# A mixer turn's three weight splits change place, and one na-gate piece on TensorE moves from attention tile 1 to tile 0

## What is computed

```
xr, kx, vx, gx, qx, mrx, mnx = split(modulate(x) @ w_in)
cr, kc, vc                   = split(modulate(ctx) @ w_in[:, :3072])
h        = rglru_bidirectional(conv4(xr), conv4(cr))        # gated recurrence, both directions
y_rnn    = h * gelu(gx)
y_na     = neighborhood_attention(rope(rms(qx)), rms(qx), rope(rms(kx)), vx, rms(kc), vc, rpb)
x        = x + m2 * ((sigmoid(mrx) * (y_rnn @ w_rnn_out) + sigmoid(mnx) * (y_na @ w_na_out)) @ w_out)
x        = x + m5 * conv_ffn(modulate(x))
```

## Time and profile before

| | |
|---|---|
| median of 3 runs | 2131.47 us (2130.02 to 2133.41) |
| the profiled execution | 2128.76 us, of which the span from first to last instruction is 2126.9 us |
| granted TensorE clock | 0.997 of full speed |
| TensorE busy | 2051.1 us (96% of the span) |
| DVE, ACT, GpSimd busy | 1628.0 (77%), 1072.5 (50%), 492.8 us (23%) |
| a stretch of 141 us over one middle turn (501 to 642 us) | TensorE 138.59 us busy, DVE 107.06, ACT 91.47, GpSimd 30.87 |

### The profile page before, as it was taken

How to read it: one execution, slowest core, us unless ns; L and a number is a source line. 1 busy time by engine, 2 the same in 40 slices (tenths; PEclk the granted TensorE clock), 3 DMA queues, 4 the chain that set the end, 5 groups by cost and what they waited for, 6 DMA issues and landing times.

```text
span 2126.9 us, 28320 instructions
## 1 busy us (share of the span) xinstructions
PE 2051.1 (96%) x10618; PEld 1739.8 (82%) x10618; DVE 1628.0 (77%) x2809; ACT 1072.5 (50%) x1631; POOL 492.8 (23%) x377
## 2 busy tenths in 40 slices
PE   5999999999999999999998899999999999999999
PEld 1878888988988889888887788887788888887887
DVE  6688598596885985859859866767998888877766
ACT  3466666665676657656666621002444334434332
POOL 0031130222212212212123010000124442115550
PEclk9999999999999999999999999999999999999999
DMA  8421211112012120120111385453347764239663
GB/s 328 112 64 41 62 51 47 47 53 70 30 41 72 40 73 20 53 70 30 43 50 69 106 310 193 144 188 131 89 134 197 183 176 118 94 122 335 226 205 126
DMA packets 105576, 241.65 MB, mean 114 GB/s; under 512 B 27264, under 2 KB 32768, under 8 KB 104960
## 3 DMA queue, kind: packets, MB, share of 16 engines
q1 hardware_dynamic: 74304, 191.08, 26.4%
q0 software_dynamic: 14592, 44.05, 8.0%
q10 hardware_dynamic: 16544, 4.72, 1.0%
HBM read 203.11 MB, written 63.96 MB: 126 GB/s over the span
## 4 chain that ended last, share of the span: by engine, by line
PE 77%; DVE 13%; ACT 4%; issue 2%; ACTq 0%; DVEq 0%
PE banks L47 14%; PE banks L49 14%; PE banks L48 14%; PE banks L991 4%; PE banks L862 4%; PE banks L864 4%; PE banks L863 4%; PE banks L895 3%; PE banks L2269 3%; PE banks L2270 3%; PE banks L2271 3%; DVE probT_low L1494 2%; PE banks L953 2%; DVE prob L1486 2%; PE banks L935 1%
## 5 line engine op out<-in xcount | busy, mean ns | idle before, releaser
L47 PE MATMUL banks<-qh,xnh 128*128 128x384 f32 (+1 forms) x640 | 223.3, 349 | 0.3 <-PEq L216 0.3
L862 PE MATMUL banks<-xnh,wh 128*128 128x512 f32 (+1 forms) x536 | 211.3, 394 | 3.2 <-ACT stage L1097 2.9
L49 PE MATMUL banks<-qh,xnl 128*128 128x384 f32 (+1 forms) x640 | 207.7, 325 | 0.0
L48 PE MATMUL banks<-ql,xnh 128*128 128x384 f32 (+1 forms) x640 | 207.6, 324 | 0.0
L864 PE MATMUL banks<-xnh,wl 128*128 128x512 f32 (+1 forms) x536 | 204.5, 381 | 0.0
L863 PE MATMUL banks<-xnl,wh 128*128 128x512 f32 (+1 forms) x536 | 204.1, 381 | 0.0
L1494 DVE TENSOR_TENSOR probT_low<-banks,probT_high 128x512 fp32r<-128x512 f32 (+2 forms) x256 | 138.9, 583 | 56.2 <-ACT probT_high L1165 55.2
L1165 ACT CAST probT_high<-banks 128x512 fp32r<-128x512 f32 (+2 forms) x256 | 117.0, 510 | 60.3 <-PE banks L953 51.4
L47 PE MATMUL banks<-yh,wh 128*128 128x512 f32 x372 | 145.0, 390 | 0.9 <-DVE wl L2471 0.9
L48 PE MATMUL banks<-yl,wh 128*128 128x512 f32 x372 | 145.0, 390 | 0.0
L49 PE MATMUL banks<-yh,wl 128*128 128x512 f32 x372 | 144.9, 390 | 0.0
(11 more groups left out here) (396 smaller groups left out, 6015.9 us busy)
## 6 DMA issues: line engine op xcount, KB each, us to landing
raw<-w_ff SPq DMA_DIRECT2D x33, 512.0 KB, 5.7
down_d<-w_down POOLq DMA_DIRECT2D x66, 256.0 KB, 6.9
raw<-w_fm SPq DMA_DIRECT2D x32, 512.0 KB, 6.7
extras<-h_d SPq DMA_DIRECT2D x55, 256.0 KB, 3.9
raw<-w_qkv SPq DMA_DIRECT2D x24, 512.0 KB, 3.9
raw<-w_mix SPq DMA_DIRECT2D x24, 512.0 KB, 4.8
h_d<-conv_d SPq DMA_DIRECT2D x21, 512.0 KB, 3.2
raw<-w_modT SPq DMA_DIRECT2D x16, 512.0 KB, 4.6
```

Of the source, the lines that this page charges most:

```text
L47: pe.matmul(out, w_hi(k), x_hi(k), start=(k == 0), stop=False)
L48: pe.matmul(out, w_hi(k), x_lo(k), start=False, stop=False)
L49: last = pe.matmul(out, w_lo(k), x_hi(k), start=False, stop=(k == chunks - 1))
L862: pe.matmul(out, fh[:, s, k, :], xnh[:, k, c0:c1], start=(k == 0), stop=False)
```

## The change

In `turn` of the five programs:

- In turns 1 to 6 the splits of XR and MR stand earlier: on ACT after the evacuation and gates of q tile 1, on DVE after `head_squares` of q tile 1.
- In turns 0 to 6 the MN split stands earlier: on ACT in front of the evacuation of MR's first half, on DVE between the normalisation of the last queries and `maxima` of tile 0. Before it stood behind the high parts of `JOBS_B` on ACT and behind their low parts on DVE.
- In turn 7 the MN split goes to q tile 1 on both engines, and `LAST_ORDER` puts MN in front of MR, with SP's wait changed to MR.
- On TensorE the piece after the scores at u = 1 is gone, and one after the scores at u = 0 is new (turns 0 to 6).

```diff
@@ -587,7 +587,7 @@
         SLOT = {XR: 0, G: 1, MR: 1, MN: 0}
         RAW = {Q0: 0, Q1: 1, Q2: 2, XR: 0, MR: 1, MN: 2, G: 0}
         ORDER = {Q0: 0, Q1: 1, Q2: 2, XR: 3, MR: 4, MN: 5, G: 6}
-        LAST_ORDER = {Q0: 0, Q1: 1, Q2: 2, MR: 3, MN: 4}
+        LAST_ORDER = {Q0: 0, Q1: 1, Q2: 2, MN: 3, MR: 4}
 
         def split_count(u, i, last=False):
             return i * UNITS + 2 + (LAST_ORDER if last else ORDER)[u] + 1
@@ -747,7 +747,7 @@
                     store_stage(smr_d, i, 1, 1)
                     store_stage(smn_d, i, 0, 2)
                     sp.wait_ge(yr_out, PAIRS * 16)
-                    sp.wait_ge(w_lo, split_count(MN, i, True))
+                    sp.wait_ge(w_lo, split_count(MR, i, True))
                     for k in range(2):
                         load_y(k)
                     sp.dma_start(raw[:, 2, :], w_mix[0]).then_inc(mix_in, 16)
@@ -1072,7 +1072,7 @@
                         mix_piece((u - 5) // 2)
                     if u + 2 < ATT:
                         scores(i, u + 2)
-                    if not last and u % 2 == 1 and u < ATT - 1:
+                    if not last and (u == 0 or u % 2 == 1 and 1 < u < ATT - 1):
                         piece()
                     if u % 2 == 0 and u >= 2:
                         weighted_values(i, u // 2 - 1)
@@ -1222,6 +1222,8 @@
                     for s in range(1, 4):
                         q_evac(i, s)
                         gate_pieces(i, *GATES_LAST[s])
+                        if s == 1:
+                            split_hi(MN, raw_count(MN, i))
                     decays(i, 0)
                     q_evac(i, 4)
                     root(i, 0)
@@ -1233,6 +1235,9 @@
                     for s in range(3):
                         q_evac(i, s, first)
                         gate_pieces(i, *GATES_AFTER[s])
+                        if s == 1:
+                            split_hi(XR, raw_count(XR, i))
+                            split_hi(MR, raw_count(MR, i))
                     decays(i, 0)
                     q_evac(i, 3)
                     q_evac(i, 4)
@@ -1240,11 +1245,10 @@
                     gate_pieces(i, *GATES_AFTER[4])
                     q_evac(i, 5)
                     gate_pieces(i, *GATES_AFTER[5])
-                if not last:
+                if first:
                     split_hi(XR, raw_count(XR, i))
-                split_hi(MR, raw_count(MR, i))
-                if last:
-                    split_hi(MN, raw_count(MN, i))
+                if first or last:
+                    split_hi(MR, raw_count(MR, i))
                 q_evac(i, 6)
                 gate_pieces(i, *(GATES_FIRST if first else GATES_AFTER)[6])
                 if first:
@@ -1522,6 +1526,11 @@
                     outputs(i - 1, GROUPS_ATT - 1, False)
                 for s in range(4):
                     head_squares(i, s)
+                    if s == 1 and last:
+                        split_low(MN, i, True)
+                    elif s == 1 and not first:
+                        split_low(XR, i)
+                        split_low(MR, i)
                 if first:
                     dve.wait_ge(const_in, 32)
                     then(dve.tensor_scalar(gqk[:, 0, :], gqk[:, 0, :], HD ** -0.5, None, ALU.mult))
@@ -1537,9 +1546,10 @@
                 if not first:
                     head_squares(i, 5)
                     mean_squares(i, 0)
-                if not last:
+                if first:
                     split_low(XR, i)
                     split_low(MR, i)
+                if not last:
                     head_squares(i, 6)
                 inverse_roots(i, 0)
                 head_norm(1, *CHUNKS[0])
@@ -1547,7 +1557,6 @@
                     head_norm(0, NCT, CHUNKS[0][1])
                     split_low(MR, i, True)
                     head_squares(i, 6)
-                    split_low(MN, i, True)
                 if first:
                     head_squares(i, 7)
                 gated_input(i, 1)
@@ -1569,6 +1578,8 @@
                 inverse_roots(i, 1)
                 normalize_keys(i, 1)
                 normalize_queries(i, 1)
+                if not last:
+                    split_low(MN, i)
                 dve.wait_ge(bias_done, i * 3 + 3)
                 for u in range(2):
                     dve.wait_ge(qk_done, i * ATT + u + 1)
@@ -1576,8 +1587,6 @@
                     maxima(i, u)
                 v_low(i)
                 tr_low(i, JOBS_B)
-                if not last:
-                    split_low(MN, i)
                 for u in range(ATT):
                     probT_low(i, u)
                     inverse(i, u)
```

## The result

The changed kernel takes **2134.57 us** (median of 21 runs, 2131.77 to 2137.85) against 2131.33 us (21 runs, 2127.7 to 2133.41) of the kernel before on the same chips: a ratio of 1.0017, 95% interval 1.0011 to 1.0023. So it is slower, surely, but by less than the 0.2% that was called the limit of what can be told. The profiled execution has a span of 2130.0 us (before 2126.9), at the same granted clock, 0.997.

The account below looks back on a forecast made before the run. TensorE, busy almost throughout, was taken as the bound, so only its waits count. Six middle turns at +0.41 us and turn 0 at +0.5 make 3.0 us slower: 2134.5 us against the median 2131.47, range 2130 to 2138.5.

Parts of the forecast that it names:

- What bounds the kernel: TensorE's 1.3 us wait at tile 1: DVE ends it, ACT nearly as late; moving MN's split alone brings some 0.2 us.
- XR's and MR's splits, turn 7: Earlier splits in turns 1 to 6 lie hidden before q tile 2; these and turn 7's changes taken as 0.
- The hold of L1489: Maxima of tile 0: L1489 ends with GpSimd's first pass, exponential 1.34 us later, tile 0 +0.74 us.
- Rival A: GpSimd doesn't hold L1489 back: tile 2 +0.11 us a turn, 2132.3 us; chance 0.12.
- From tile 0 to tile 2: Middle turns: tile 1 follows tile 0 after 2.69 us, tile 2 after 2.53 more, so +0.41 us a turn.
- The bound from the middle turn's own chain: Alternative for tile 0 to tile 1: 2.53 plus 0.05 us, tile 1 at 595.01, giving +0.30 us a turn.
- The sum: Six middle turns at 0.41 us plus 0.5 us in turn 0: 3.0 us slower, 2.2 by the lower bounds.
- from there the order on all engines is the old one: Behind tile 2 TensorE is packed and the old order holds, so nothing gives the +0.41 us a turn back.
- Turn 0: Both GpSimd passes follow each other and L1489 ends with them; tile 2 at 176.19 instead of 175.69, +0.5 us.
- Rival B: The wait at tile 1 is simply filled, qpS in time: -0.44 us a turn, 2128.4 us; chance 0.08.
- C: Rival: GpSimd's second pass gets in before L1489; +1.52 us in each of six turns, 2141.1 us; chance 0.08.
- D: Rival: later tile 0 also lengthens waits at the weighted values, another 0.3 us a turn; 2136.6 us; chance 0.10.

Follow-up runs that it names:

- e10: Kernel before with the piece moved and only one of 1024 columns of MN's low part made in turns 0 to 6: 2128.16 us, ratio 0.9984.
- e8: Kernel before with only the piece moved from u = 1 to u = 0: 2128.4 us, ratio 0.9987.
- e1: Changed kernel with MN's split (turns 0 to 6) and the piece at their old places: 2130.59 us, ratio 0.9997.
- e4: Changed kernel with DVE's MN subtraction between the maxima of tiles 0 and 1: 2131.26 us, ratio 1.0005.
- e3: Changed kernel with the piece back at u = 1: 2137.91 us, ratio 1.0032.
- e5: e4 with GpSimd's second sigmoid pass waiting for the maxima of tile 1: 2128.8 us, ratio 0.9987.
- e6: Changed kernel with GpSimd's first sigmoid pass waiting for the maxima of tile 0: 2130.54 us, ratio 0.9995.
- e7: Changed kernel with the small instruction ending the maxima given one tensor input and a pointer scalar, all tiles: 2135.87 us, ratio 1.0017.
- e2: Kernel before with only MN's split (turns 0 to 6) and the piece moved: 2134.69 us, ratio 1.0014.
- e9: Changed kernel with the one-input form of the small instruction for tile 0 alone: 2134.07 us, ratio 1.0008.

## Why the prediction was right, and where it was off

**What bounds the kernel.** Right. The wait at tile 1 was a wait with two ends 0.2 us apart, and the most that taking DVE's end away brings, besides the piece, is e10 against e8: tile 0 to tile 1 takes 2.58 instead of 2.79 us, and the turn 140.13 instead of 140.35 on average, 0.22 us.

**XR's and MR's splits, turn 7.** Taken as 0, measured as 0 (e1). In the changed kernel q tile 2's evacuation starts at 528.48 us, 0.77 later than in the earlier trace rows, and the rstd row at 551.13, 0.78 later. That is what had been lost up to there (tile 2 of turn 2 is 0.71 us later than before, and tile 3 behind it 0.08 more), so nothing was lost in between. ACT's idle time in front of that evacuation is 1.65 us instead of 3.54: the casts lie in it.

**The hold of L1489.** Right in place and size. Worked out was the exponential at 586.29, which is 1.83 us after that turn's `stage` (L1097 of MR's first half, at 584.46); in the changed kernel `stage` is at 585.21, and 587.05 - 585.21 = 1.84 us. Tile 0 was worked out at 592.43 - 584.46 = 7.97 us after `stage`, and starts at 593.20 - 585.21 = 7.99. Beside the two meetings of the earlier trace rows there are now four more, each ending within 0.02 us of the pass (the middle turn and turn 0 of the changed kernel, tile 1 in e4, and e3's with 589.56 + 0.59 = 590.15 beside 589.10 + 1.04 = 590.14). And three ways of taking the meeting away (e5 and e6 move the pass, e7 the second input) each give the 0.16 or 0.21 us. The Trainium skill's page "SBUF — State Buffer", section "SBUF: two separate sides", has the reason, that the port which DVE shares with GpSimd is locked for the length of an instruction and that a DVE instruction with two SBUF inputs asks for it. The traces agree: with two inputs it ends with the pass, and the one-input form of e7 takes 0.21 us in the middle of one. Rival A (no hold) falls.

**From tile 0 to tile 2.** Worked out as 2.69 and 2.53 us; both are measured so (595.89 - 593.20 and 598.42 - 595.89). The bound from the middle turn's own chain, 2.58, was rightly not taken. The reason given for it, that ACT has come to rest before, falls with e5: there ACT works up to the casts (`stage` from 592.47 to 593.07, the casts from 592.96), and tile 0 to tile 1 still takes 2.72 us. What else could be the reason stands in the last section; it is not shown.

**The sum.** Worked out was +0.41 us a turn, measured is +0.485. The term that was left out lies behind tile 2: from there to tile 3 it is 601.73 - 598.42 = 3.31 us, and before it was 3.23 (600.47 - 597.24). The step "from there the order on all engines is the old one" was right for the order and 0.08 us short in time: tile 2, which TensorE used to reach late, now has to be waited for, and behind a wait TensorE starts anew. In e8 it is 3.30 us (599.62 - 596.32), with a wait at tile 2 and every other part of the change undone. That is 6 x 0.08 = 0.5 us, a sixth of the sum.

**Turn 0.** The event worked out for it happened: both passes one after the other, L1493 ending with the second. Worked out was +0.5 us, measured +0.45 between the two profiled executions; e2's has +0.34. What the working did not see is that turn 0 has a second order, with `stage` ahead, which e1, e3, e7, e9 and e10 fell into. There tile 2 starts 14.9 to 16.9 us after `stage`, so which order an execution falls into counts for more than this term, and the small instruction meets the second pass even where the subtraction has not moved (e1, e10).

**The time.** 2134.5 us was predicted, 2134.57 measured. Part of that closeness is luck: up to tile 2 of turn 7 the rows have 0.45 + 2.91 + 0.14 = 3.5 us where 3.0 were forecast, and medians of the kernel before alone lie between 2131.3 and 2131.9 in these comparisons. The changed kernel's own times also go with the granted clock, from 2132.9 us on average at 0.997 (five executions) to 2136.3 at 0.994 (six). Rival B (the wait simply filled) fell, and its price was nearly right for a case that the change doesn't reach (e10: -0.38 us a turn, worked out as -0.44). C (the second pass wins) happened in turn 0 only, as said; in the experiments it also happened in turn 0 of e1, e2 and e10 and at tile 1 in e4. D (the chain grows at the weighted values) didn't happen here, the waits are the 1.1 us of before; it did in e7, where DVE's work in the loop grew.

## What to carry to other kernels

A wait that is ended by one engine with another 0.2 us behind it is worth 0.2 us, whatever is taken away from the first; work out the second before moving anything. Work that is moved "to a free place" on an engine without gaps shifts what is behind it: look for who needs the very next small instruction, and for which instruction of another engine it will now fall into. And if a change has two parts, price each alone: here one line brought 0.15 us a turn, and what came with it cost 0.66. Count the waits too, not only their sum: each one costs more than the profile shows for it.

## What was not expected of the hardware

- A DVE instruction on 128 x 1 elements with two tensor inputs took 0.58, 0.88 and 0.98 us instead of 0.16 when it fell into GpSimd's 1.04 us pass. The profile shows no wait for it: it shows a longer instruction. The one-input form took 0.21 us in the same place.
- The exponential of tile 1 starts 0.73 us after ACT's casts of tile 0 begin in the kernel before, e8 and e10, and 0.88 to 0.89 us in e4, e5, the changed kernel and turn 7 of before. In the first three DVE's `qrS` has ended when the casts start (594.09 against 594.18 in e10), in the others it is still reading (593.23 against 592.96 in e5). This is what e5 lacked of its expected turn, 0.13 us. That DVE's reading of PSUM beside the casts is the cause fits these seven places, but no run changed it alone, and it fits turn 0 less well: in before, e8 and e10 `qrS` ends 0.06 us after the casts start and the exponential still comes after 0.72 to 0.73 us, in e7 it ends 0.09 us after and it is 0.89. Another difference fits all of them: where it is 0.73 us, MN's subtraction (in e10 its one column) stands between `qrS` and the first `probT_low`. So the cause is open.
- Each wait of TensorE costs about 0.24 us more than its length in the profile: 0.16 us of drain that counts as busy, and up to 0.08 us behind it. Worked out from rows of the changed kernel, it also fits others: in e3 the waits are 0.46 us more than before with one wait more, 0.70 us (measured +0.66); in e10 0.63 less with one more, -0.39 (measured -0.38); in e5 0.48 less with one more, -0.24 (measured -0.24). In e6, which by its view has 0.54 less with one more, it fails, -0.30 (measured +0.07), until the wait at tile 0 that the view doesn't list is counted: 0.29 us late, 0.16 of it drain, so 0.13 + 0.24 more, +0.07. In e8, 0.52 less with one more, it gives -0.28 where -0.15 was measured; what is missing there wasn't found.
